# The short convolution of tiles 2 and 3 as a stage of its own beside the choice of tile 1, with its weights loaded a second time

## The reference

```python
def shortconv_branch(sb, sc, sx, conv_w, w_out):
    return (sb * causal_dwconv(sc * sx, conv_w)) @ w_out
```

```python
    u = expert_u[eidx]
    v = expert_v[eidx]
    act = jax.nn.gelu(jnp.einsum('td,thkd->thk', xb, u).astype(jnp.float32), approximate=False)
    return jnp.einsum('thk,thkd->td', (g * act).astype(v.dtype), v)
```

## Time and profile before

| | us |
|---|---|
| median of 3 runs | 2383.35 |
| lowest, highest | 2379.07, 2385.44 |
| span of the profiled execution | 2541.9 |
| TensorE busy in it | 2151.2 (85%) |
| VectorE busy in it | 1499.3 (59%) |
| POOL busy in it | 1020.5 (40%) |
| bytes read from memory in it | 835.70 MB |

### The profile page before, as it was taken

How to read it: one execution, slowest core, us unless ns; L and a number is a source line. 1 busy time by engine, 2 the same in 40 slices (tenths; PEclk the granted TensorE clock), 3 DMA queues, 4 the chain that set the end, 5 groups by cost and what they waited for, 6 DMA issues and landing times.

```text
span 2541.9 us, 29123 instructions
## 1 busy us (share of the span) xinstructions
PE 2151.2 (85%) x10694; PEld 1516.7 (60%) x10694; DVE 1499.3 (59%) x3505; ACT 653.7 (26%) x1838; POOL 1020.5 (40%) x1028
## 2 busy tenths in 40 slices
PE   8999998999999986996675366276879799999998
PEld 7999785666666975874431254221366555545695
DVE  3441179999999368647454677710067665886321
ACT  6772235566555121001010101110122000001220
POOL 0000014555665113435566554566544544772000
PEclk8999999999998997998886567578887899999999
DMA  6767568999999978999999888999978998998485
GB/s 237 245 231 240 215 254 298 404 397 393 390 377 337 378 274 320 398 356 380 363 394 361 308 335 320 366 343 364 409 307 323 411 348 313 412 412 355 157 316 173
DMA packets 196750, 839.81 MB, mean 330 GB/s; under 512 B 22000, under 2 KB 22384, under 8 KB 164864
## 3 DMA queue, kind: packets, MB, share of 16 engines
q0 software_dynamic: 147456, 536.94, 54.8%
q1 hardware_dynamic: 43808, 290.72, 30.6%
q10 hardware_dynamic: 5344, 10.29, 1.3%
HBM read 835.70 MB, written 2.16 MB: 330 GB/s over the span
## 4 chain that ended last, share of the span: by engine, by line
PE 60%; DVE 15%; issue 10%; ACT 6%; POOL 5%; another core or an unknown queue 3%; DMA 2%; ACTq 0%; DVEq 0%; SPq 0%
PE ps L1200 59%; DVE rows L2745 7%; POOL rows L1172 5%; DVE ps L2769 1%; DMA rows<-in_pv,eidxT 1%; DVE h L2769 1%; DVE arena L2297 1%; DMA wr<-in_wso 1%; ACT arena L1734 1%; ACT L1871 1%; ACT arena L1865 0%; DMA wr<-in_wgate 0%; ACT L1801 0%; DVE arena L2359 0%
## 5 line engine op out<-in xcount | busy, mean ns | idle before, releaser
L1172 POOL DMA_INDIRECT rows<-in_pu,eidx x512 | 485.3, 948 | 936.6 <-DVE dots L2745 368.7
L1200 PE MATMUL ps<-arena,wr 128*128 128x128 f32 (+4 forms) x3968 | 771.9, 354 | 26.0 <-DMA wr<-in_wso 9.2
L1200 PEld LDWEIGHTS ps<-arena,wr 128*128 128x128 f32 x3968 | 606.9, 195 | 168.6 <-issue 27.3
L2745 DVE CUSTOM_DVE_ANT_0 rows<-rows,ps 128x1024 f32<-128x1024 f32 x512 | 594.0, 1217 | 11.3 <-DMA rows<-in_pu,eidx 5.5
L1200 PE MATMUL ps<-hT,wr 128*128 128x128 f32 (+2 forms) x1600 | 369.7, 390 | 44.6 <-issue 41.3
L1172 POOL DMA_INDIRECT rows<-in_pv,eidx x256 | 289.2, 1130 | 207.0 <-DVE h L2769 101.4
L1200 PEld LDWEIGHTS ps<-hT,wr 128*128 128x128 f32 x1600 | 262.5, 199 | 148.7 <-issue 57.6
L1172 POOL DMA_INDIRECT rows<-in_pv,eidxT x256 | 245.7, 960 | 142.9 <-issue 68.6
L1200 PE MATMUL ps<-rows,wz 128*32 128x512 f32 x1024 | 180.7, 778 | 78.5 <-DMA rows<-in_pv,eidxT 57.1
L1200 PE MATMUL ps<-wr,arena 128*128 128x256 f32 (+2 forms) x704 | 180.7, 412 | 2.1 <-ACT arena L1943 2.1
L2769 DVE SCALAR_TENSOR_TENSOR h<-rows,wgt,h 128x1024 f32<-128x1024 f32 x132 | 169.0, 1280 | 5.7 <-DMA rows<-in_pv,eidx 4.8
(11 more groups left out here) (403 smaller groups left out, 2258.3 us busy)
## 6 DMA issues: line engine op xcount, KB each, us to landing
wr<-in_wg SPq DMA_DIRECT2D x48, 1024.0 KB
wr<-in_wgu SPq DMA_DIRECT2D x33, 1024.0 KB
wr<-in_wgate SPq DMA_DIRECT2D x24, 1024.0 KB
wr<-in_wso SPq DMA_DIRECT2D x24, 1024.0 KB
wr<-in_wq SPq DMA_DIRECT2D x16, 1152.0 KB
wr<-in_wsc SPq DMA_DIRECT2D x16, 1024.0 KB
wr<-in_wqku SPq DMA_DIRECT2D x15, 1024.0 KB
wr<-in_wdn SPq DMA_DIRECT2D x14, 1024.0 KB
```

The costliest lines, as they stand in the source:

```text
L1172: e.indirect_dma_start(ring[slot_of[i]], None, A[table], bass.IndirectOffsetOnAxis(ap=index[:, t, k:k + 1], axis=0)).then_inc(gathered[slo ...
L1200: return e.matmul(o, l, r, start=start, stop=stop, skip_group_check=True)
L2745: e.tensor_tensor_reduce(row, row, wide[:], 1.0, 0.0, MUL, ADD, dots[:, k:k + 1]).then_inc(*dve.up(*u))
```

## The change

The short convolution is split at tile 1. In the scan of tiles 1 to 3 its products, taps and results cover 128 columns, those of tile 1. The 256 columns of tiles 2 and 3 are a new stage `short, 2` (`plan_short`), ahead of the y turns and sums of these tiles and merged with tile 1's choice in their place, after the first gate product. It loads `wsc` again (16 loads, 12.6 MB), takes banks from `hi`, `hi` and `lo`, and has buffers `sx` and `sy` behind the sums' buffers of tiles 2 and 3. Its history is the `hsc` that tile 1 left. `QUOTA` changes with it: in seven steps of the scan 3 rows fewer each; 14 more in the sums and 7 more in the query of tile 1; 38 in the new stage (0, 5, 10, 12, 11 over its fifths); in the attention, heads and output of tiles 0 and 1, 18, 7 and 17 fewer. Tile 0 and scan 0 are as before. Of `QUOTA`'s one line only the stages that change are shown.

```diff
-('mixer', 1, 1): (7, 12, 11), ('mixer', 1, 2): (12, 4, 7, 11), ('mixer', 1, 3): (5, 11, 6, 8), ('mixer', 1, 4): (11, 13, 9), ('mixer', 1, 5): (10, 11, 9), ('mixer', 1, 6): (9, 5, 7, 14), ('mixer', 1, 7): (6, 12, 7)
+('mixer', 1, 1): (7, 9, 11), ('mixer', 1, 2): (9, 4, 7, 11), ('mixer', 1, 3): (5, 8, 6, 8), ('mixer', 1, 4): (11, 10, 9), ('mixer', 1, 5): (10, 8, 9), ('mixer', 1, 6): (9, 5, 7, 11), ('mixer', 1, 7): (6, 9, 7)
-('sum', 1): (12,), ('query', 1): (6,)
+('sum', 1): (26,), ('query', 1): (13,)
-('attend', 0): (29, 19, 4, 3, 0, 0, 18, 29), ('heads', 0): (2, 10, 21, 18, 26), ('wout', 0): (44, 1, 5, 4, 5, 7)
+('attend', 0): (24, 15, 4, 0, 0, 0, 16, 25), ('heads', 0): (2, 10, 19, 17, 22), ('wout', 0): (32, 1, 3, 4, 5, 4)
+('short', 2): (0, 5, 10, 12, 11)
+def short_parts(s):
+
+    return ((0, 0, 144, META), (1, 0, 128, 0), (1, 128, 256, 0))[s]
...
+def short_units(pl, A, s, j, rings="lo lo lo"):
+    n = short_parts(s)[2]
+
+    def product(s_):
+        if s_ == 2:
+            pl.load(("wsc", s, j, 0), A["wsc"][j, :, 0:2048], 2048, ("pe", "sprod", s, j, 1))
+        elif s_ == 0:
+            pl.load(("wsc", s, j, 1), A["wsc"][j, :, 2048:3072], 1024, ("pe", "sprod", s, j, 0))
+        pl.take(("sprod", s, j, s_), rings.split()[s_], {2: ("act", "keepx", s, j), 1: ("dve", "times", s, j),
+                                                         0: ("dve", "short", s, j)}[s_])
+        pl.add("sprod", s, j, s_, p=mmc(n))
...
+def plan_short(pl, A):
+    pl.stage = ("short", 2)
+    units = [u for j in range(8) for u in short_units(pl, A, 2, j, "hi hi lo")]
+    for k in range(len(units) + 1):
+        if k < len(units):
+            units[k][0]()
+        if k:
+            units[k - 1][1]()
+        yield True
+    pl.stage = ("late", 2)
...
-        lead = (group_units(step) if step < G else []) + (short_units(step - 1) if step else [])
+        lead = (group_units(step) if step < G else []) + (short_units(pl, A, q, step - 1) if step else [])
...
-        yield from merge(pl, (choose[1], 0.001), (sums[2], CY))
+        yield from merge(pl, (choose[1], 0.001), (itertools.chain(plan_short(pl, A), sums[2]), CY))
...
-            lay(S[2], arena, after, sum_parts(2))
+            o = lay(S[2], arena, after, sum_parts(2))
+            lay(S[2], arena, o, [("sx", [128, 258]), ("sy", [128, 256])])
...
-                               m["uT"][:, k, off:n], k == 0, k == 7)
+                               M[q]["uT"][:, k, first + off:first + n], k == 0, k == 7)
...
-                        w.wait_ge(*dve.at("short", scan_of(q), 7))
+                        w.wait_ge(*dve.at("short", q, 7))
...
-                    e.tensor_copy(hsc[:, j, :], x[:, n:n + 2]).then_inc(*dve.up())
+                    if s < 2:
+                        e.tensor_copy(hsc[:, j, :], x[:, n:n + 2]).then_inc(*dve.up())
```

More of the change, by code:

```diff
@@ L1093, in up_of, with short_y @@
             return AT[t0][f"up{j % 2}" if f"up{j % 2}" in AT[t0] else "up0"]
+        def short_y(s):
+            return S[2]["sy"] if s == 2 else M[s]["tmpy"]
         def yh_of(q, c, g):
@@ L1328, in tensor @@
                 elif kind == "sprod":
-                    _, q, j, s_ = u
-                    m = M[q]
-                    nt, m0, n, nr, chunks = group(*SCANS[q])
+                    _, s, j, s_ = u
+                    q, first, n, m0 = short_parts(s)
                     off = m0 if s_ == 0 else 0
-                    wt = weights("wsc", q, j, 0 if s_ else 1)
+                    wt = weights("wsc", s, j, 0 if s_ else 1)
                     so = 1024 if s_ == 1 else 0
@@ L2821, in build @@
         for u in pl.units:
-            if u[0] in ("conv", "times"):
+            if u[0] == "conv" or u[0] == "times" and u[1] < 2:
                 mine = [x for x in xp_of if x[1] == u[1]]
```

70 lines of the change are left out of this document (31 added, 39 removed).

## The result

The changed kernel takes 2464.61 us (median; 2453.59 to 2468.14), the kernel before beside it 2383.76 us: ratio 1.0329, 95% interval 1.0301 to 1.0358. It is 81 us slower where 8 us less were forecast (9 of the span), and outside the range of 2338 to 2406.

A forecast was written before the change was run, and what follows sets the result against it. It took TensorE, VectorE and transfers as all nearly full in the scan, with TensorE idling in tile 1's choice. -42 + 5 + 78 - 50 = -9 us of the span, scaled by 0.938 to -8: 2375 us, range 2338 to 2406.

The forecast's parts named there:

- part 3: New stage and sums of tiles 2 and 3: the added products, only partly hidden beside tile 1's choice, cost +78 us.
- lower end of +53: New stage and sums of tiles 2 and 3: cost if TensorE filled all its 33 idle us with the 86.
- part 4: After the sums of tiles 2 and 3: 38 fewer rows left, -50 us, ends -32 and -70.
- part 1: Scan of tiles 1 to 3: TensorE loses 85 us, VectorE 34, and VectorE's limit decides: -42 us.
- part 2: Sums and query of tile 1: 14 and 7 added rows, VectorE's work in the sums hidden, transfers mostly: +5 us.
- the signs that the prediction named: Scan about 395 us, VectorE over 0.95, TensorE near 0.83; tile 1's sums within 8 of 83; output products 41 later.
- the -30 of the bytes: Scan: 21 rows fewer are 11 MB, at the scan's transfer rate -30 us.
- +6 for h3's latency: Choice of tile 3, 1308 to 1434 us: cost of some 34 dot products of tile 2 coming beside it.
- The gaps of 22.61 and 38.86 us: TensorE's waits late in the profile: the first would go or move into the sums, the second would go.
- A: New stage and the sums behind it: transfers bound, +16 us, so 2398; chance 0.27.
- B: Whole kernel: the scan gives only -32, the rest as forecast, +1 us, so 2384; chance 0.10.
- C: Whole kernel: TensorE stays fed in the choice, scan -48, both gaps close, -48 us, so 2338; chance 0.18.

The follow-up runs named there:

- second profile: The kernel before, unchanged, profiled again: 2384.64 us, span 2382.8 against 2541.9 in the execution that the prediction read.
- half dot products: Changed kernel with all quotas of the kernel before, VectorE's dot products of tile 0 over 512 of 1024 columns, gathers whole: 2465.79 us.
- light loads: Changed kernel with all quotas of the kernel before, the scan's 16 loads of short convolution weights cut to 32 columns: 2458.65 us.
- dealing only: Kernel before with only the new row numbers of the scan, the sums and the query of tile 1, no split: 2397.55 us, 1.006.
- split only: Changed kernel with every number of `QUOTA` as in the kernel before: 2472.85 us, 1.0377.
- half the rows: Kernel before with the row numbers of the scan's eight dealing steps halved: 2560.76 us; the same with the split: 2569.87 us.

## Why the prediction was wrong

**What bounds the kernel.** The reading that the scan has three nearly full resources was right, and it should have decided the sum. The reading that TensorE idles in tile 1's choice (29 of 70 us, and 33 us to the end of the sums) was that of an execution 159 us longer than the next; the second profile has 14 us idle of 68 from 932 to 1000, 16 to the end of the sums, and 17 in the whole stretch. The warning stood in the profile: a span 6.7% over the median, and two long waits released by "issue". Scaling the sum by 0.938 was no remedy, since the extra time was not spread evenly. This misreading made the change look better founded than it was, but it is not what the sum failed by: part 3 counted only 8 of the 86 us of products as hidden, and the 33 us stand in its lower end of +53 alone.

**The misses by size.** Forecast -9, measured +78.3 between the spans. Of the 87 us between them part 4 makes 36, part 3 33, part 1 15 and part 2 4. Of the signs that the prediction named, the scan came near (398 us and TensorE 0.85, but VectorE 0.93 and not over 0.95) and the sums of tile 1 missed by 1 us (8.6 longer than in the second profile); the output products, but for their last 4.3 us, ended 92 us later and not 41, and TensorE did wait for `in_wsc`, though only 9.7 us.

**Part 1, the scan: -42 forecast, -27.4 measured.** The step that failed is "now VectorE's decides: 416 - 34 = 382 us busy, with its 21 us of idle time cut by 8". VectorE's busy time fell by 38 us (406.9 to 369.1), more than the 34 forecast, but its idle time did not shrink by 8: it grew by 11 (18 of 425 us to 29 of 398). By itself the split gives 2.2 us and the dealing 12.8; only together do they give 27.4. By count of VectorE's row products in the traces the scan lost 24 rows (232 to 208) and not 21, since the weighted sum is dealt four rows at a time; 27.4 us are 1.14 a row. The prediction's other value, the -30 of the bytes, was near, and the runs with half dot products and light loads show that the transfers (0.96 busy, 374 GB/s) are close behind VectorE. But they are not seen to stop it in this stretch: VectorE waits for no gathered row there, and its longest waits are for ACT, 3.9, 3.7, 3.4 and 2.7 us (L1895, L1906, L1872, L1818). What makes up the 11 us is not shown.

**Part 2: +5 forecast, +8.6 measured**, inside its bounds of 0 and 20. The same 8.0 us came in dealing only.

**Part 3: +78 forecast, +110.5 measured**, and above its upper end of 94. It comes apart by the runs without the split and without the 38 rows: the split costs 324.0 - 248.2 = 75.8, the rows dealt ahead 15.4, the 38 rows 19.3 (23.6 with the 4.3 us of output products that they push behind the cut). The price of the products was about right: TensorE's busy time in the stretch grew by 85 us where 86 were forecast, although a 256-column record took 409 ns on average where the new products stand (913 to 1055 us), against 386.

```profile
L1225 PE MATMUL ps<-arena,wr 128*128 128x256 f32 x355 | 87.2, 409 | 25.8 <-DVE arena L2341 12.2 <-DMA wr<-in_wsc 9.7 <-DVE arena L2359 4.0
```

The 75.8 us for 86 us of work was foreseen too. Mis-sized were the rows: 7 rows ahead of the choice were given +8 and the 38 in it -9, together about nothing, and they measured +35. The +8 counted VectorE's own time for 7 rows. By the trace of dealing only 8 more row products stand there (12 for 4), their gathered rows have not landed when VectorE comes to them (7.0 us of waiting), and TensorE waits 14.2 us for the first scores. The -9 was for 21 dot products beside the choice instead of 29. By count the 38 rows put 35 more dot products into the whole stretch (120 for 85 without them), and these stand in front of `times` and `short`, which free the banks that TensorE waits for: 16.2 us of such waits in the changed kernel, none without the 38 rows. TensorE is the engine that sets this stretch, so it pays for them.

**Part 4: -50 forecast, -13.7 measured** (+27.2 - 46.4 + 5.5). This is the largest miss. It comes apart by the run without the 38 rows: the rows change the three stretches by +20.4, -48.4 and +4.3 us, -24 together, and the split with the rows dealt ahead adds 10. The stretch to the attention of tile 2 gave what 38 rows are worth: 19.9 MB at 407 GB/s are 49 us, 46.4 measured. But the prediction counted "+6 for h3's latency" for dot products of tile 2 beside tile 3's choice. They were 38 more, VectorE worked alone for 77 of 78 us there, and TensorE's gap grew from 14.9 to 77.9 us. That step failed: of what the rows save later, 20 us are lost again ahead of the attention. The gaps of 22.61 and 38.86 us went much as forecast: they are 17.91 and 33.50 in the second profile, the first moved into the end of the sums and is 11.35 us, the second is gone, and a new one of 24.68 us at tile 2's weights' turn (2.73 before) stands for it. The last two are part of the 46.4; the first lies ahead of that stretch.

**The rivals.** A put the loss on transfers. As a mechanism it was half right, and its place was wrong: the transfers hold the scan together with VectorE (half the dot products: 384 GB/s, 53.3 us of waiting for gathers), and by their rate (1.02 busy, 405 and 407 GB/s) and TensorE's 92.3 us of waiting for gathered rows they hold the two stretches up to the attention of tile 2, though no run took bytes alone away there. In the new stage they don't (0.82 busy, 315 GB/s without the 38 rows), and taking the second load away gave 8 us. None of the rivals was the one that happened: the work taken from the scan is worth almost nothing there (2.2 us for the split alone), and costs 76 of its 86 us in the new place. That second half stood in the forecast; the first half, and that dealt rows are not free where they are put, did not. B and C both took the scan's gain for granted.

The Trainium skill, DMA: Bandwidth & Descriptors, section Bandwidth, puts the limit on the memory side at about 358 GB/s per core, and gives 425 for one large transfer with the pair's other core idle. The second profile of before holds 405 and 407 GB/s for 259 and 332 us. So 358 did not limit this kernel, which runs on one core, and the rates lie under the 425, which the page also measured with one core.

## What to carry to other kernels

An engine that is 95% busy in a stretch need not be what bounds it: before work is moved out, ask what else there is at that height, and count the gain down to the next bound only. And price work that is dealt into another stretch by what it holds up there, not by its own time: here 8 row products ahead of the choice made TensorE wait 14 us for the first scores, and rows beside the new stage held its banks. The cheapest run that decides it is the one that thins that engine's work in place (here 6 of 8 matmuls of each product gone, a ratio of 0.9999) and so shows what the source stretch pays before anything is built at the destination. And compare a profile's span with the timed median first; if they differ by more than the timed runs do, idle time read from it is not the kernel's.

## What was not expected of the hardware

One execution of the same program had 159 us more span than the next, with a wait of ACT of 19.05 us for a queue that the trace doesn't name and TensorE's of 16.64 us behind it, while the timed runs spread over 6 us (2379 to 2385). TensorE's mean granted clock was 0.97 in the scan before, 0.88 with the products thinned, where it waited 65.6 us for the scan's state (33.4 and 32.2), and 1.00 with half the rows, when it was busy 393 of 397 us (1 is the level of 2.4 GHz, the other level is 1.2). So part of what was taken from it came back as slower matmuls in these runs. The thinned products are 96 us by the count of records, but its busy time in the scan fell by 61; the 343 us at 0.88 are worth 311 at 0.97, which is the missing rest. The forecast's 85 us of TensorE came back as 59 in the same way (split only, 0.89).
